# Attention output in two PSUM banks, its deviation by logarithm, another order of the last S5 block, and router logits summed inside the output projection

## What is computed

```python
xn = rms_norm(h, mix_norm_g)
q_a, k_a, v_a, u_s5, q_h, f_h, i_h, g_h = split(xn @ w_in)          # 5504 columns
mix = concat(diff_attention(q_a, k_a, v_a), s5_mixer(u_s5), hgrn2_mixer(q_h, f_h, i_h, g_h))
h = h + mix @ w_out                                                # 2048 -> 2048
hn = rms_norm(h, ffn_norm_g)                                       # the router reads this
# hier_moe: 4 groups of 8 experts
gl, el = hn @ w_group, hn @ w_router                               # 4 and 32 logits a token
g_idx = argmax(gl); p_g = softmax(gl)[g_idx]
top_vals, top_idx = top_k(el of that group, 2); gates = softmax(top_vals) * p_g
h = h + sum over the two experts of gate * (silu(hn @ w_gate) * (hn @ w_up)) @ w_down
out = rms_norm(h, final_norm_g)
```

## Time and profile before

| | us |
|---|---|
| median of 3 runs | 2055.41 (2052.52 to 2056.9) |
| the profiled execution, its own time | 2060.28 |
| its span | 2058.4 |
| TensorE busy | 1906.0 (93%) |
| VectorE busy | 821.7 (40%) |
| ACT busy | 259.6 (13%) |
| GpSimd busy | 189.1 (9%) |
| HBM read | 504.26 MB |

### The profile page before, as it was taken

One profiled execution on the slowest core, in us unless ns is written; L12 is line 12 of the kernel. 1 busy time (PEld: TensorE's weight loads), 2 busy tenths in 40 slices (PEclk: granted clock), 3 DMA queues, 4 the chain that ended last, 5 costly groups with the idle time before them and its releaser, 6 DMA issues.

```text
span 2058.4 us, 32623 instructions
## 1 busy us (share of the span) xinstructions
PE 1906.0 (93%) x13671; PEld 1183.1 (57%) x13671; DVE 821.7 (40%) x1531; ACT 259.6 (13%) x626; POOL 189.1 (9%) x218
## 2 busy tenths in 40 slices
PE   6999999999998979998468999999999999999996
PEld 4888999699987869998122333333333323333332
DVE  6666685176465543333511222212222312222215
ACT  3012112100334231112000000000000000000002
POOL 1353332000000000000010000000000000000000
PEclk9999999999999999999689999999999999999998
DMA  5243333211121233222299999999999999999992
GB/s 208 88 141 99 83 94 96 91 52 60 64 72 47 67 128 109 82 83 78 92 423 425 425 422 423 420 419 422 414 421 406 423 422 411 424 411 423 420 387 105
DMA packets 74419, 508.53 MB, mean 247 GB/s; under 512 B 19200, under 2 KB 19348, under 8 KB 38176
## 3 DMA queue, kind: packets, MB, share of 16 engines
q1 hardware_dynamic: 56720, 486.34, 58.4%
q0 software_dynamic: 5728, 15.81, 2.3%
q10 hardware_dynamic: 11824, 4.17, 1.1%
HBM read 504.26 MB, written 12.99 MB: 251 GB/s over the span
## 4 chain that ended last, share of the span: by engine, by line
PE 77%; DMA 13%; DVE 5%; issue 3%; ACT 2%; SPq 0%; POOL 0%; DVEq 0%; ACTq 0%; POOLq 0%
PE psum L1124 19%; PE psum L843 19%; PE psum L846 15%; DMA arena<-in_moe_w_gate 11%; PE psum L1086 9%; PE psum L1143 6%; PE psum L988 2%; DVE arena L1422 2%; DMA arena<-in_moe_w_down 1%; PE psum L900 1%; PE psum L1099 1%; PE psum L1048 1%; DMA arena<-hs_rows,arena 1%; DVE arena L1425 1%; PE psum L977 0%
## 5 line engine op out<-in xcount | busy, mean ns | idle before, releaser
L1124 PE MATMUL psum<-arena 128*32 128x512 f32 x4096 | 465.9, 608 | 32.6 <-issue 15.9
L843 PE MATMUL psum<-arena 128*128 128x128 f32 x3584 | 411.0, 277 | 2.6 <-issue 2.6
L843 PEld LDWEIGHTS psum<-arena 128*128 128x128 f32 x3584 | 407.8, 194 | 4.1 <-issue 3.6
L1422 DVE TENSOR_TENSOR arena<-psum,arena 128x512 f32<-128x512 f32 x290 | 198.9, 689 | 417.1 <-PE psum L1086 413.9
L1124 PEld LDWEIGHTS psum<-arena 128*32 128x32 f32 x4096 | 135.1, 112 | 355.4 <-issue 354.2
L846 PE MATMUL psum<-arena 128*128 128x256 f32 x1456 | 324.7, 382 | 1.9 <-DVE arena L521 1.4
L846 PEld LDWEIGHTS psum<-arena 128*128 128x128 f32 x1456 | 275.1, 191 | 40.7 <-issue 3.9
L1422 DVE TENSOR_TENSOR arena<-arena,psum 128x256 f32<-128x256 f32 (+2 forms) x174 | 76.5, 439 | 434.9 <-PE psum L843 206.9
L1086 PE MATMUL psum<-arena 128*128 128x512 f32 x512 | 236.0, 605 | 0.9 <-issue 0.9
L1143 PE MATMUL psum<-arena 128*32 128x512 f32 x2048 | 225.9, 599 | 5.7 <-DMA arena<-in_moe_w_down 5.3
L1422 DVE TENSOR_TENSOR arena<-arena 128x128 f32<-128x128 f32 (+17 forms) x448 | 180.1, 443 | 39.8 <-ACT arena L1203 31.3
(11 more groups left out here) (187 smaller groups left out, 989.1 us busy)
## 6 DMA issues: line engine op xcount, KB each, us to landing
arena<-in_moe_w_gate SPq DMA_DIRECT2D x64, 2048.0 KB, 26.7
arena<-in_moe_w_up SPq DMA_DIRECT2D x64, 2048.0 KB, 26.4
arena<-in_moe_w_down SPq DMA_DIRECT2D x64, 2048.0 KB, 26.3
arena<-in_w_in SPq DMA_DIRECT2D x86, 512.0 KB, 4.6
arena<-in_w_out SPq DMA_DIRECT2D x32, 512.0 KB, 4.7
arena<-in_x SPq DMA_DIRECT2D x8, 1024.0 KB, 8.2
hs_rows<-arena SPq DMA_DIRECT2D x4, 1024.0 KB, 4.0
out<-arena SPq DMA_DIRECT2D x4, 1024.0 KB, 4.0
```

Source lines behind the costliest of these rows:

```text
L843: last = mm(B(bank, [(1, P)], off=t * P), F(a + t * P, P), F(w + i * P, P), start=start and t == 0, stop=(i == KH - 1), skip_group_check=True)
L1124: last = mm(B(bank, [(1, FE)], 32 * g, 32), F(XT + c * CAP + 32 * g, 32), F(SLOT[slot] + (c % 8) * FE, FE), start=(c == 0), stop=(c == KD ...
L1422: return v.tensor_tensor(o, a, b, op)
```

## The change

Five things are done.

1. At the start: a Sqrt is run on a constant before x arrives; the first pair's first two weight sums are made before the discretisation; the sum S4 is made in one operation behind the first chunk's product.
2. The last S5 block's `y5`, `yt` and `ge` come 1, 3 and 3 gaps earlier (the last `ge` was bound to the last gap, so it comes one gap earlier).
3. Attention: a head's output goes to bank 3 or 2 in turn, the small steps choose from banks 0, 1 and spare ones; the deviation is taken as exp(-0.5 ln(mean + eps)), so VectorE's reciprocal goes.
4. Router: h is transposed unscaled, two column chunks per pair of the output projection, one pair late (`ht`), and its logits are added in bank 3 (`lg`), the two chunks in two halves of the partitions; `rT` adds the halves and turns them by a selection matrix. The gain is multiplied into the router's weights, and into the experts' transposed rows (`turned`, table G2). The 1/deviation is applied to the logits. The rows for memory are scaled by ACT, without the gain, in three buffers.
5. The ranking is made on TensorE by three small products (`rc` counts and compares, `ro` the order, `rr` the ranks), and comes before the gates.

```diff
-        JUNK, SSP = AQ + 4 * HB, AQ + 4 * HB + P
+        JUNK, SSP = AQ + 4 * HB, AQ + 5 * HB
-        HNT = SLOT[6]
-        GF, HSB = E0 + 2048, [E0, E0 + 4096]
+        HSB = [E0, E0 + 2048, E0 + 4096]
+        HTB, RLT = VG, VG + 4 * S
-        WR = W - KD * 36
+        WR = S2
...
+            y_at, yt_at, ge_at = (10, 14, 17) if more_ else (9, 11, 14)
...
-        for p in WO_P:
-            gaps += products(p)
+        for i, p in enumerate(WO_P):
+            g = products(p)
+            if i:
+                g[1] += [("ht", i - 1, 0), ("ht", i - 1, 1)]
+                g[3].append(("lg", i - 1))
+            gaps += g
+        gaps.append([("ht", 7, 0), ("ht", 7, 1), ("lg", 7)])
-        steps += [("hT", t, q) for t in range(TB) for q in range(4)]
-        steps += [("rt",), ("rT",), ("rk",), ("id",)]
+        steps += [("rT",), ("rc",), ("ro",), ("rr",), ("rk",), ("id",)]
...
-                small, ticking = [0, 1, 2], True
+                small, ticking = [0, 1], True
...
+            elif s[0] == "w4":
+                spare = [5, 6, 7]
             elif s[0] == "pe":
-                spare = []
+                spare = ([5, 6, 7], [6, 7], [], [])[s[1]]
...
-                bank = 3
+                bank = 3 - s[1] % 2
... SyncE: the router's weights with x, before the output projection
-                elif blocks[i][0] == ("wo", 4, 0):
-                    see_copy(sp, ("az", AH - 1))
-                    see_copy(sp, ("pr", WO_P[0], 6))
-                    sp.dma_start(F(WR, KD * 36), DV(d["router"], ...)).then_inc(router_in, 16)
-                    sp.dma_start(F(GF, D), DV(d["ffn_norm_g"], ...)).then_inc(gf_in, 16)
+                    sp.dma_start(F(WR, NWR), DV(d["router"], ...)).then_inc(router_in, 16)
... TensorE
+                if kind == "lg":
+                    i = s[1]
+                    if i == 0:
+                        take_bank(pe, s)
+                        once(router_ready, 1)
+                    for c in range(2):
+                        once_copied(("ht", i, c))
+                        last = mm(B(3, [(1, S)], 64 * c, 64), F(WR + (2 * i + c) * 64, 64), F(HTB + (2 * (i % 2) + c) * S, S),
+                                  start=(i == 0), stop=(i == 7), skip_group_check=True)
+                    last.then_inc(full[3] if i == 7 else lg_done, 1)
+                    return
+                elif kind == "ht":
+                    i, c = s[1:]
+                    for n in (4, 5, 6):
+                        once_copied(("pr", WO_P[i], n))
+                    for t in range(TB):
+                        last = tr(B(bank, [(1, P)], off=t * P), F(H0 + t * D + (2 * i + c) * P, P), ident)
                 elif kind == "rT":
-                        last = tr(B(bank, [(1, 36)], off=t * 36), F(RLT + t * P, P, 0, 36), F(IDENT, 36, 0, 36))
+                        last = mm(B(bank, [(1, 36)], off=t * 36), F(RLT + t * P, P), F(WRS, 36), start=True, stop=True)
+                elif kind == "rc":
+                    for i in range(2):
+                        for t in range(TB):
+                            counts, ones = F(AS + t * NE, NE), F(C["ones"], NE)
+                            last = mm(B(bank, [(1, NE)], 0, NE, off=i * NE), (counts, ones)[i], (ones, counts)[i],
+                                      start=(i == 0 and t == 0), stop=(t == TB - 1), skip_group_check=True)
+                elif kind == "ro":
+                    last = mm(B(bank, [(1, NE)], 0, NE), F(EIDM, NE, 0, NE), F(ROH, NE, 0, NE), start=True, stop=True)
+                elif kind == "rr":
+                    last = mm(B(bank, [(1, NE)]), F(C["ones"], P, 0, NE), F(RDG, NE, 0, NE), start=True, stop=True)
... ACT
+            A(F(SM, 1), F(EPSC, 1), ACT.Sqrt)
...
-                              for t in range(TB): one Square of 128 columns at each j
+                                A(F(JUNK, 2 * P), F(H0 + t * D + j * P, 2 * P), ACT.Square,
+                                  accum_out=F(SSP + t * 8 + i, 1)).then_inc(squares_done, 1)
...
-                    deviation([...], F(ASQ, P), SM + 20, HST + TB, AV, R0 + (h % 2) * TB).then_inc(ao_std, 1)
+                    squares([...], F(ASQ, P), SM + 20, R0 + (h % 2) * TB)
+                    A(F(HST + TB, TB), F(SM + 20, TB), ACT.Ln, scale=1.0 / AV, bias=F(EPSC, 1)).then_inc(act_step, 1)
+                    act.wait_ge(act_step, n_step[0])
+                    A(F(HST + TB, TB), F(HST + TB, TB), ACT.Exp, scale=-0.5).then_inc(ao_std, 1)
...
+            act.wait_ge(h_rst, 1)
+            for t in range(TB):
+                if t == 3:
+                    act.wait_ge(hs_out[0], 16)
+                A(F(HSB[t % 3], D), F(H0 + t * D, D), ACT.Copy, scale=F(RST + t, 1)).then_inc(hs_ready, 1)
... VectorE
-                settle(v.reciprocal(F(HST + TB, TB), F(HST + TB, TB)))
...
+                        weight_sum(dve, v, 0, 0)
+                        weight_sum(dve, v, 0, 1)
                         disc_a()
...
+                elif s == ("pj", "u", 0):
+                    dve.wait_ge(xsum_ready, 1)
+                    tt(F(S4, KH * HB), F(A12, KH * HB), F(S2, KH * HB), SU).then_inc(xsum_ready, 1)
...
+                elif kind == "ht":
+                    if i == 0 and c == 0:
+                        dve.wait_ge(router_in, 16)
+                        tt(V(WR, [(64, KD), (1, 64)]), V(WR, [(64, KD), (1, 64)]), V(WRG, [(1, KD), (0, 64)]),
+                           M).then_inc(router_ready, 1)
+                    if i >= 2:
+                        dve.wait_ge(lg_done, i - 1)
+                    bank = see_bank(dve, s)
+                    v.tensor_copy(F(HTB + (2 * (i % 2) + c) * S, S), B(bank, [(1, S)])).then_inc(free[bank], 1)
+                elif s == ("lg", 7):
+                    dve.wait_ge(squares_done, 8 * TB)
+                    v.tensor_reduce(F(SSQ, TB), V(SSP, [(8, TB), (1, 8)]), AX.X, AD).then_inc(squares_sum, 1)
+                    bank = see_bank(dve, s)
+                    v.tensor_copy(F(RLT, S), B(bank, [(1, S)])).then_inc(free[bank], 1)
+                    dve.wait_ge(h_std, 1)
+                    v.reciprocal(F(RST, TB), F(STD, TB)).then_inc(h_rst, 1)
... VectorE, behind the one-hots
+            settle(v.scalar_tensor_tensor(F(RKY, NE, 0, NE), B(bank, e32, 0, NE, off=NE), float(NE), F(FE_, NE, 0, NE), M, SU))
+            v.scalar_tensor_tensor(F(RNB, NE, 0, NE), B(bank, e32, 0, NE), float(NE), F(RKY, NE, 0, NE), M, ALU.is_lt)
+            settle(v.tensor_reduce(F(RKC, 1, 0, NE), F(RNB, NE, 0, NE), AX.X, AD))
+            ts(F(ROH, NE, 0, NE), F(RKOF, NE, 0, NE), F(RKC, 1, 0, NE), None, ALU.is_equal).then_inc(ranks_ready, 1)
+            ts(F(RDG, NE, 0, NE), F(IDENT, NE, 0, NE), F(RKC, 1, 0, NE), None, M).then_inc(ranks_ready, 1)
+            v.tensor_copy(F(ORD, NE, 0, 1).bitcast(I32), B(bank, e32, 0, 1)).then_inc(free[bank], 1)
...
-            the ranking over 32 x 32 elements (lines 1930 to 1933 and 1938 to 1941)
...
-                    v.tensor_copy(F(XT + 4 * f * CAP, 4 * CAP), B(TURN_BANK[f], [(1, 4 * CAP)])).then_inc(xT_free, 1)
+                    tt(V(XT + 4 * f * CAP, [(CAP, 4), (1, CAP)]), B(TURN_BANK[f], [(CAP, 4), (1, CAP)]),
+                       V(G2 + 4 * f, [(1, 4), (0, CAP)]), M).then_inc(xT_free, 1)
```

More of the change, by code:

```diff
@@ L231, in build @@
             take(n) for n in (NE, NE, NE, NAS, NAS, NAS, NAS, NE * NE, NOV + 1))
-        RKY, RRK, RNB, RSQ, RCP, RBS, RORD = (take(NE) for _ in range(7))
+        RKY, RRK, RNB, RSQ, RCP, RBS, ROH, RDG = (take(NE) for _ in range(8))
+        RKC = take(1)
         RKS, RPX = take(TB * NE), take((TB + 1) * NE)
-        assert at[0] <= WR
+        assert at[0] <= W
         XG, YSB, XT = [E0, E0 + 2048], E0 + 4096, E0 + 6144
@@ L858, in do @@
                         once(xsum_ready, 2)
+                    elif p == 0 and n == 6:
+                        once(xsum_ready, 3)
                     if p == WO_P[0]:
@@ L1205, in _, with squares @@
             n_step = [0]
-            def deviation(srcs, junk, ss, sd, width, scales=None):
+            def squares(srcs, junk, ss, scales=None):
                 for i, x in enumerate(srcs):
@@ L1213, in deviation @@
                     act.wait_ge(act_step, n_step[0])
+            def deviation(srcs, junk, ss, sd, width):
+                squares(srcs, junk, ss)
                 return A(F(sd, len(srcs)), F(ss, len(srcs)), ACT.Sqrt, scale=1.0 / width, bias=F(EPSC, 1))
@@ L1336, in do @@
                         act.wait_ge(ao_ready, h)
-                    deviation([B(bank, [(1, P)], off=t * P) for t in range(TB)], F(ASQ, P), SM + 20, HST + TB, AV,
-                              R0 + (h % 2) * TB).then_inc(ao_std, 1)
+                    squares([B(bank, [(1, P)], off=t * P) for t in range(TB)], F(ASQ, P), SM + 20, R0 + (h % 2) * TB)
+                    A(F(HST + TB, TB), F(SM + 20, TB), ACT.Ln, scale=1.0 / AV, bias=F(EPSC, 1)).then_inc(act_step, 1)
+                    n_step[0] += 1
+                    act.wait_ge(act_step, n_step[0])
```

(15 more changed lines are left out.)

144 lines of the change are left out of this document (70 added, 74 removed).

## The result

The kernel after took **2044.28 us** (median of 6 runs, 2042.15 to 2048.26), the one before 2055.29 beside it (6 runs, 2052.07 to 2059.35): ratio 0.9943, 95% interval 0.993 to 0.9957. It is 11.0 us faster where 44.8 were forecast, and lies outside the range. Its profiled execution took 2043.22 us, span 2041.4.

A forecast was written before the change was run, and what follows sets the result against it. TensorE was taken to bound the kernel until about 1000 us, then the expert weights' stream; gains 4.0 + 6.5 + 9.0 + 19.2 + 6.1 = 44.8 off 2060.28 gave 2015.5, less 4.9 to the median: 2010.6 us, range 1999 to 2027.

The forecast's parts named there:

- Part 1: Start of the kernel: table loads leave the first block's path and VectorE's sums move; gain 4.0 us (0 to 4.5).
- Part 2: Last S5 block: an earlier Gelu closes the gap before the GLU product and its slow clock; gain 6.5 us.
- Part 4: Router inside output projection: 32.8 us gained after it, 13.6 added inside; net gain 19.2 us (13 to 22).
- Part 5: From one-hots to order: ranking on TensorE takes 5.0 us instead of 11.1; gain 6.1 us (4.3 to 8).
- rival D: Expert stream waits for its slots (4.6 us) or two logits chunks run in sequence (6.0): 2016 to 2017; chance 0.18.
- Rival E: Output projection: added work grows by stalls, 16 copies each holding TensorE 2.6 us; no change, 2052 us; chance 0.03.
- Part 3: Attention: two output banks end a wait, Ln and Exp sharing a table set drop a load; gain 9.0 us.
- Rival B: Attention: Ln's set lacks Exp, two loads per head stay; gain about 0.5 us, not 9.0: 2019 us; chance 0.27.
- Rival C: Attention: TensorE waits for a logits bank in each of 24 steps, 48 us lost: 2059 us; chance 0.04.
- the first part: The prediction's opening on what bounds the kernel: TensorE up to about 1000 us, then the expert weights' stream.
- The second half: From first expert weight transfer (1019.60 us) on: moves as a whole, so every microsecond won before arrives at the end.
- the working for 641.41: Attention: of 6.0 us at one output-bank wait only 1.4 come back, as TensorE then waits for VectorE.

The follow-up runs named there:

- experiment 5: Kernel before with 108 already-met waits (54 instructions) put at TensorE's start: 2063.67 us, ratio 1.0033 to before.
- experiment 1: Changed kernel with the attention's Sqrt and reciprocal back, its new banks kept: 2038.35 us, ratio 0.9915 to before; attention stretch 203.9 us.
- Experiment 2: Changed kernel with one output bank and three small banks back, Ln and Exp kept: 2040.3 us, ratio 0.9929 to before; attention stretch 203.5 us.
- experiment 3: Changed kernel with both attention edits undone (banks and deviation as before): 2031.28 us, ratio 0.9876 to before; attention stretch 196.6 us.
- experiment 4: Changed kernel with 124 already-met waits (62 instructions) ahead of TensorE's program: 2033.2 us, ratio 0.9888 to before.
- experiment 6: Changed kernel with both attention edits undone and 62 dead instructions ahead of TensorE's program: 2020.21 us, ratio 0.9822 to before.
- experiment 8: Changed kernel with both attention edits undone and 64 already-met waits (32 instructions) ahead of TensorE's program: 2055.0 us, ratio 0.9986 to before.

## Why the prediction was wrong

**Right.** Part 1: 5.5 for 4.0; the third product began at 48.08, 1.2 us sooner than the working had it. The first chunk alone took 13.97 us, where it was kept at 15.59. Part 2: 6.8 for 6.5, by both of its terms. Part 4: the logits are in place 5.6 us after the end of the last sum (predicted 6.0, from terms that add up to 6.3). The added work inside the projection cost 14.6 (predicted 13.6). Of this, seven pairs at 0.87 + 1.01 make 13.2 (predicted 1.94 a pair), and the two chunks of a pair do run beside each other. The other 1.4 lie in the products beside them: 64 records take 7.24 us from start to start (929.57 to 936.81), and 7.16 at before's 187.84 us for 1680. The net gain, 18.6 for 19.2, owes 4.5 to the profiled execution of before; against one like experiment 5 it is 14.1. What the Trainium skill (TensorEngine Tiling (Array Packing), "Key Properties") says of draining at a change of the tiling mode is borne out that far: two records' time of 0.86 came to 1.01 with the going back and forth. Part 5: order 2.6 us after the one-hots for 5.0, since all 16 small records took 1.03 together; 1.3 of it went to a later first transfer, whose cause was not tried. The stream did not run dry: its rate stayed at 391 GB/s or more between 1028 and 1060 us, and the first slots were handed back 42.2 us after the first transfer (predicted 41.5), so that half of rival D is out, as is its other half. Rival E is out too: no waits in the projection.

**Part 3 is the step that failed:** +9.0 forecast, -12.4 measured, 21.4 us, outside its own lower bound of -3. It has two halves. With only the logarithm in, the attention is 6.8 us longer than with neither, and with only the banks 7.3 (experiments 1 to 3).

*The table load.* "By Ln and Exp, if both are in the table set that the softmax's Exp uses, that load goes": it does not go. The trace shows a load before the Ln and one before the Exp after it. Rival B had this right (0.27), and its price was too small: it put the later deviation against the banks' gain and came to +0.5, though its own premise is a load of 1.28 plus an instruction in VectorE's way at each of four places, 4 x 1.5 = 6; 5.3 was measured by experiment 1. The rule of the Trainium skill that was weighed there (ScalarE: Activation LUTs, "Table sets: the hidden batching unit": ln followed by exp costs one load) does not hold for this kernel: the trace has two loads in each of the six heads. Why the set with both functions was not chosen is not shown. The row that spoke against it, a Square given a set without the Sqrt that followed, was the better guide.

*The banks.* The 13.5 us of waits went, as forecast, but "a head's last transpose can wait for VectorE to empty a logits bank, about 0.5 us in five heads" was too little by far. The four rows of waits in the trace after hold 27.1 us, with single ones of 8.8, 4.1 and 3.5. Experiment 2 gives the net: 5.7 lost where 1.4 x 4 less 2.5, some 3, were to be won. Rival C names this mechanism; it was priced for 24 steps at 2 us, and given its small form only as the lower bound. What the working missed is the order in ACT's queue: the copy that empties a bank of transposed weights (L1235) stands behind the next unit's exponentials, and these wait for VectorE's maximum of that unit's logits. The next transposes wait for the bank as long as that takes, not as long as one copy (2.89 us at 607.04). It is not the deviation's second load that makes this wait, as it is 2.89 us with Sqrt too (experiment 1); with a third bank it is gone, though ACT is as late (experiment 2). The three rows of waits for VectorE, 19.4 us, are what the Sqrt shortens, to 12.7. How much of the 5.7 each place has was not tried. (In the working for 641.41, TensorE comes 6.5 us sooner without the bank wait, not 6.0; the 1.4 that it counts are not touched by that.)

**The second failed step** stands in the first part: "The second half therefore moves as a whole with its first transfer". It gave back 8.9 us. Experiments 4, 5, 6 and 8 show that this comes from the place of the loop in TensorE's program, which every added instruction ahead of it moves: the place cost before 9.9 us in experiment 5, and with another place the changed kernel won back 7.2 in experiment 4.

**The third is small:** the profiled execution of before was taken as 4.9 above the median, and that of after was assumed to be so as well; it was 1.1 below. That is 6.0 us, and no mechanism of the change. Of the 4.9, 4.5 lay in the router's part of that one execution (39.2 us against 34.7 in experiment 5).

By the steps, between the profiled executions: +1.5 (part 1), +0.3 (2), -21.4 (3), -0.6 (4), +1.1 (5), -8.9 (second half), -6.0 (profiled execution and median) make -34.0, against the 33.7 us by which the forecast of 2010.6 was missed.

## What to carry to other kernels

Before counting on a shared table set, look in a trace for what is loaded between the two functions; where it isn't shared, keep the function whose successor loads its table beside VectorE's next step, as Sqrt did. Taking a bank from a group that is filled and emptied at every step cost more here than giving one to a place that was waited for four times brought: count who empties the bank, and what is queued ahead of that. And when a change to a kernel with a loop loses time in a part that it does not touch, shift the loop by some dead instructions first: here that was worth 11 us to the kernel after, and between the worst and the best of the places tried 35.

## What was not expected of the hardware

A jump back to the loop's start costs TensorE some 4 us each time (5 stops, 20.4 us in experiment 6), and a second stop follows when few of the block's instructions are left behind the target: 4.3 to 4.6 us with about 12 left, between nothing and 3.0 with 44, none with 98 (before) or 238 (experiment 6). These counts are estimates: two instructions to a record ahead of the second stop, then the 54 and 62 instructions of the shifts, and blocks of 256. (The expectations count one more, 45 and 13.) The five stops themselves remain in the best version, and nothing here was tried against them.
